# The adaLN modulation of a hybrid trunk layer: two parts as columns on the turned tokens, four parts inside the input projection

## What is computed

```python
mod = silu(c) @ w_ada + b_ada                      # 1024 -> 6 * 1024, for c and for c_ctx
sh1, sc1, g1, sh2, sc2, g2 = split(mod, 6)
h = rms_norm(x, norm1) * (1 + sc1) + sh1
proj = h @ w_in + b_in                             # qa ka va (384 each), qb kb vb ob (384 each), 16 gates, 256 pool
mixed = concat(attention, sigmoid(ob) * mlstm, pool) @ w_out
x = x + g1 * mixed
h2 = rms_norm(x, norm2) * (1 + sc2) + sh2
x = x + g2 * moe(h2)
```

## Time and profile before

| | |
|---|---|
| median of 3 runs | 1669.62 us (1667.91 to 1673.24) |
| profiled execution, its own time | 1669.87 us |
| its span | 1668.2 us |
| TensorE matmuls busy | 1419.5 us, 85% of the span |
| TensorE weight loads | 794.5 us, 48% |
| VectorE busy | 595.0 us, 36% |
| ScalarE busy | 314.8 us, 19% |
| GpSimd busy | 159.3 us, 10% |
| bytes moved by DMA | 222.54 MB, mean 133 GB/s |

### The profile page before, as it was taken

The page is one execution under the profiler, slowest core; times in us unless marked ns, Lnnn a source line. Parts: engine busy times, 40 slices in busy tenths (PEclk is TensorE's granted clock), DMA queues, the critical chain, the costliest instruction groups (busy, mean ns, idle before and its releaser), DMA issues. The chain is left out here.

```text
span 1668.2 us, 16922 instructions
## 1 busy us (share of the span) xinstructions
PE 1419.5 (85%) x5847; PEld 794.5 (48%) x5848; DVE 595.0 (36%) x1173; ACT 314.8 (19%) x681; POOL 159.3 (10%) x167
## 2 busy tenths in 40 slices
PE   5798999999988999866769975079998999999952
PEld 1124555555567788755634432044444444444521
DVE  0242136011111666568922246322232332323217
ACT  0310000033001444433511111011111111111123
POOL 0003000000000111025200000410001000000030
PEclk9998999999998999968979987589999999999977
DMA  8767411110003221001060025337758669577144
GB/s 318 252 239 240 44 38 38 38 38 3 25 33 71 36 39 20 21 11 58 2 239 0 0 63 206 131 130 264 259 203 326 236 237 318 207 278 280 38 180 178
DMA packets 121015, 222.54 MB, mean 133 GB/s; under 512 B 38217, under 2 KB 48121, under 8 KB 120829
## 3 DMA queue, kind: packets, MB, share of 16 engines
q1 hardware_dynamic: 104995, 172.16, 31.3%
q0 software_dynamic: 9664, 32.30, 5.5%
q10 hardware_dynamic: 6304, 17.37, 2.8%
HBM read 194.31 MB, written 30.43 MB: 135 GB/s over the span
## 5 line engine op out<-in xcount | busy, mean ns | idle before, releaser
L485 PE MATMUL ps<-sb 128*128 128x512 f32 (+1 forms) x576 | 189.5, 492 | 1.9 <-PEq L314 1.9
L488 PE MATMUL ps<-sb 128*128 128x384 f32 (+1 forms) x576 | 172.8, 463 | 0.0
L485 PEld LDWEIGHTS ps<-sb 128*128 128x128 f32 x576 | 95.8, 192 | 96.3 <-issue 95.8
L488 PEld LDWEIGHTS ps<-sb 128*128 128x128 f32 x576 | 109.2, 190 | 62.3
L1669 PE MATMUL ps<-sb 128*128 x256 | 120.9, 628 | 13.4 <-ACT sb L1713 13.4
L1229 PE MATMUL ps<-sb 128*128 128x512 f32 x288 | 126.3, 597 | 0.0
L1642 PE MATMUL ps<-sb 128*128 x256 | 115.3, 604 | 1.2 <-ACT sb L1701 1.2
L1646 PE MATMUL ps<-sb 128*128 x256 | 112.5, 592 | 0.0
L209 PE MATMUL ps<-sb 128*2 128x512 f32 x192 | 88.7, 618 | 25.9 <-DMA sb<-in_w_ada 17.3
L1749 DVE TENSOR_SCALAR sb<-sb 128x512 f32<-128x512 f32 (+1 forms) x32 | 11.5, 359 | 270.3 <-ACT sb L1706 236.9
L1229 PEld LDWEIGHTS ps<-sb 128*128 128x128 f32 x288 | 54.7, 192 | 65.9 <-issue 65.9
(11 more groups left out here) (295 smaller groups left out, 1745.4 us busy)
## 6 DMA issues: line engine op xcount, KB each, us to landing
sb<-in_w_gate SPq DMA_DIRECT2D x16, 2048.0 KB, 8.5
sb<-in_w_up SPq DMA_DIRECT2D x16, 2048.0 KB, 15.9
sb<-in_w_down SPq DMA_DIRECT2D x32, 1024.0 KB, 10.0
sb<-in_w_ada SPq DMA_DIRECT2D x12, 2048.0 KB, 8.0
sb<-in_w_in SPq DMA_DIRECT2D x7, 1536.0 KB, 7.1
slot_y<-sb ACTq DMA_DIRECT2D x16, 512.0 KB, 6.5
sb<-mod_rows SPq DMA_DIRECT2D x6, 1024.0 KB, 11.2
sb<-in_x_all ACTq DMA_DIRECT2D x9, 512.0 KB, 6.5
```

Of the source, the lines that this page charges most:

```text
L485: last = nc.tensor.matmul(bank(i % 8)[0:m, 0:tn], w[:, k, b * m:(b + 1) * m], hT[:, k, t0:t0 + tn], start=(k == 0), stop=(k == KD - 1))
L488: last = nc.tensor.matmul(bank(i % 8)[:, 0:m], hT[:, k, t0:t0 + P], w[:, k, 0:m], start=(k == 0), stop=(k == KD - 1))
```

## The change

- The vectors c, b_ada's first 2048 elements and norm1 come in as rows of 128 and are turned once to columns.
- Parts 0 and 1 are made as columns: the 128x128 blocks of w_ada's first 2048 columns are stationary, the two columns of silu(c) move. w_ada comes in eight row blocks of 1 MB with four semaphores; block k from the fifth on waits for the product of block k - 4.
- The token tiles come in three transfers of three. Each batch is squared, scaled by its inverse root in place, turned, and copied by ScalarE and VectorE half each.
- Scale and shift are then applied to `hT`, whose partitions are channels: eight passes over 1024 latent columns (three on ScalarE, five on VectorE), and eight over the 128 context columns.
- All this is at the head of the projection's block; blocks 1 and 2 are gone.
- Parts 2 to 5 are made in eleven pieces of up to 384 columns, inserted as units 12, 16, 20 and so on. A piece is four column groups of 32 stationary columns (two of them are used) and 96 moving columns each. Each piece's weights go to `w_first`, free after qa. The results go to `mod_rows` as they come.
- The order of the groups becomes qa, ka, va, qb, vb, ob, kb, tail, and the sigmoid's work moves under kb. `rpb_rows` is written once unit 8 is done.
- The scale of the second norm is made from the repeated rows in the output projection.

```diff
-        def multiply_ada(pe, n):
-            pe.wait_ge(ada_loaded[n % 2], 16 * (n // 2 + 1))
...
-                last = nc.tensor.matmul(bank(2 + n % 2)[0:2], cc[:, :, k], ada[n % 2][:, k, :],
-                                        start=(k == 0), stop=(k == KD - 1))
...
+        groups = [("T", C_QA, AW), ("T", C_KA, AW), ("N", C_VA, AW), ("S", C_QB, MW), ("N", C_VB, MW), ("N", C_OB, MW),
+                  ("S", C_KB, MW), ("N", C_TAIL, TAIL)]
+        GATE_GROUP = 5
+        PIECE = 4 * 96
+        n_pieces = -(-4 * D // PIECE)
+        piece_cols = lambda j: min(PIECE, 4 * D - j * PIECE) // 4
...
+        for j in range(n_pieces):
+            units.insert(NT + 3 + 4 * j, ("mod", j, 4 * 32, 0, piece_cols(j)))
...
+        early = [sb[:, early_at[k % 7]:early_at[k % 7] + 2 * D] for k in range(KD)]
...
+            for k in range(KD):
+                if k >= 4:
+                    sp.wait_ge(ada_mm, k - 3)
+                sp.dma_start(early[k], w_ada[k * P:(k + 1) * P, 0:2 * D]).then_inc(ada_in[k % 4], 16)
+                if k in (0, 2, 4):
+                    load_x(k // 2)
+            sp.dma_start(w_first, w_src[:, :, C_QA:C_QA + AW]).then_inc(w_first_in, 16)
+
+        def front_act(act):
+            st = act_steps.on(act)
+            act.dma_start(ident, k_ident).then_inc(const_ready, 16)
+            act.wait_ge(vec_copied, 1)
+            nc.scalar.activation(ce, vec_cols[:, 0:2 * KD], ACT.Exp, scale=-1.0).then_inc(silu_exp, 1)
+            for n in range(3):
+                act.wait_ge(x_in[n], 16)
+                tiles = range(BATCH1 * n, BATCH1 * (n + 1))
+                for t in tiles:
+                    if t:
+                        act.wait_ge(squares, t)
+                    nc.scalar.activation(sq_junk, x_res[:, t, :], ACT.Square, accum_out=ss[:, t:t + 1]).then_inc(squares, 1)
+                b = slice(BATCH1 * n, BATCH1 * (n + 1))
+                act.wait_ge(mean_ready, n + 1)
+                nc.scalar.activation(y0[:, b], ss[:, b], ACT.Sqrt).then_inc(guess_ready, 1)
+                for t in tiles:
+                    act.wait_ge(turned, t + 1)
+                    nc.scalar.activation(hT[:, 4:8, t * P:(t + 1) * P], bank(2 * (t % 3) + 1).rearrange("p (k t) -> p k t", k=4),
+                                         ACT.Copy).then_inc(copied_act, 1)
...
+            for k in DVE_KS:
+                nc.vector.tensor_scalar(hT[:, k, 0:LAT], hT[:, k, 0:LAT], mods[:, KD + k, 0:1], mods[:, k, 0:1],
+                                        ALU.mult, ALU.add).then_inc(mod_dve, 1)
...
+            def multiply_ada(k):
+                pe.wait_ge(ada_in[k % 4], 16 * (k // 4 + 1))
+                for b in range(2 * KD):
+                    last = nc.tensor.matmul(bank(6)[:, 2 * b:2 * b + 2], early[k][:, b * P:(b + 1) * P], cc[:, k, 0:2],
+                                            start=(k == 0 and b == 0), stop=(k == KD - 1 and b == 2 * KD - 1))
+                last.then_inc(ada_mm, 1)
+
+            def turn_x(n):
+                for t in range(BATCH1 * n, BATCH1 * (n + 1)):
+                    pe.wait_ge(scaled, t + 1)
+                    if t >= 3:
+                        pe.wait_ge(copied_act, t - 2)
+                        pe.wait_ge(copied_dve, t - 2)
+                    for k in range(KD):
+                        at = 2 * (t % 3) * BANK + k * P
+                        last = nc.tensor.transpose(ps[:, at:at + P], x_res[:, t, k * P:(k + 1) * P], ident)
+                    last.then_inc(turned, 1)
+
+            for step in (0, 1, 2, "x0", 3, "x1", 4, 5, "x2", 6, 7):
...
+                for i in range(len(units)):
...
+                            sp.dma_start(wring[g % 2][:, :, 0:n], w_src[:, :, c0:c0 + n]).then_inc(w_loaded[g % 2], 16)
+                    if i == last_of[0]:
+                        sp.dma_start(rpb_rows, bass.AP(rpb_pad.tensor, 0, [[PADW, HEADS * RPB_R], [0, GRID_W], [1, PADW]])).then_inc(mod_stored[0], 16)
+                    for j in range(n_pieces):
+                        if i == (piece_at[j - 1] if j else last_of[0]):
+                            sp.wait_ge(proj_mm, i + 1)
+                            at, n = 2 * D + j * PIECE, 4 * piece_cols(j)
+                            sp.dma_start(w_piece[:, :, 0:n], ada_src[:, :, at:at + n]).then_inc(piece_in, 16)
...
+                    if g == "mod":
+                        pe.wait_ge(piece_in, 16 * (b + 1))
+                        for k in range(KD):
+                            for q in range(4):
+                                last = nc.tensor.matmul(bank(i % 8)[32 * q:32 * q + 32, 0:tn], cc[:, k, :], w_piece[:, k, q * tn:(q + 1) * tn],
+                                                        start=(k == 0), stop=(k == KD - 1))
+                        last.then_inc(proj_mm, 1)
+                        continue
...
+                dve.wait_ge(n2_rows_in, 48)
+                st.link(nc.vector.scalar_tensor_tensor(out=n2_rows[0], in0=n2_rows[0], scalar=1.0, in1=bc(n2_w[:, None, :], (P, 2, D)),
+                                                       op0=ALU.add, op1=ALU.mult))
                 dve.wait_ge(sq2, 1)
```

More of the change, by code:

```diff
@@ L174, in program @@
         mark_h = ar.at
[L175 to L192, removed]
-        dve_steps, act_steps = Steps(None, sem("dve_steps")), Steps(None, sem("act_steps"))
[L194 to L202, removed]
-        def multiply_ada(pe, n):
-            pe.wait_ge(ada_loaded[n % 2], 16 * (n // 2 + 1))
-            if n >= 2:
-                pe.wait_ge(mod_evac, n - 1)
-            for k in range(KD):
-                last = nc.tensor.matmul(bank(2 + n % 2)[0:2], cc[:, :, k], ada[n % 2][:, k, :],
-                                        start=(k == 0), stop=(k == KD - 1))
[L211 to L222, removed]
+        dve_steps, act_steps = Steps(None, sem("dve_steps")), Steps(None, sem("act_steps"))
+        mod_stored = [sem("mod_stored0"), sem("mod_stored1")]
         def newton(st, y, t, ms):
@@ L229, in newton @@
             st.link(nc.vector.scalar_tensor_tensor(out=y, in0=t, scalar=1.5, in1=y, op0=ALU.add, op1=ALU.mult))
[L231 to L287, removed]
@@ L299, in load_rows_of, with norm_stage @@
                 sp.dma_start(row, mod_row(part)).then_inc(loaded, 16)
[L301 to L311, removed]
+        def norm_stage(tag, x, rinv, nat, outT, sp_more, pe_more, dve_last, pool_more, rows):
+            (scale_row, shift_row), row_loaded = rows
             nat_ready, turned, copied = (sem(tag + n) for n in ("nat_ready", "turned", "copied"))
-            nat_of = lambda t: two[t % 2] if ring else nat[:, t, :]
             with nc.Block() as block:
@@ L316, in _ @@
                 def _(sp):
[L317 to L320 removed]
+                    sp_more(sp)
                 @block.scalar
@@ L423, in program @@
         after_attention_in = ar.at
+        pin_at = ar.at
         pin = ar.take([NT, PW])
@@ L451, in program @@
         sig_exp, zeros_ready = sem("sig_exp"), sem("zeros_ready")
+        x_res = sb[:, mark_h:mark_h + NT * D].rearrange("p (t d) -> p t d", t=NT)
+        early_at = [after_proj, after_proj + KD * AW] + [kaT_at + n * 2 * D for n in range(3)] + [mark_h + NT * D + n * 2 * D for n in range(2)]
+        assert early_at[-1] + 2 * D <= qaT_at and early_at[4] + 2 * D <= pin_at
+        early = [sb[:, early_at[k % 7]:early_at[k % 7] + 2 * D] for k in range(KD)]
+        small = Arena(sb, after_proj)
@@ new lines, in program @@
+        small.at = pin_at
+        vec_rows, vec_cols = small.take([P]), small.take([40])
+        ce, cc = small.take([2 * KD]), small.take([KD, 32])
+        mods = small.take([2 * KD, 2])
+        ss, y0, nt1 = (small.take([NT]) for _ in range(3))
+        brow = small.take([n_pieces * (PIECE // 4)])
+        mrow = [small.take([PIECE // 4]) for _ in range(2)]
+        sq_junk = sb[:, block_at:block_at + D]
+        vec_in, vec_turned, vec_copied, silu_exp, silu_done = (sem(n) for n in ("vec_in", "vec_turned", "vec_copied", "silu_exp", "silu_done"))
```

217 lines of the change are left out of this document (143 added, 74 removed).

## The result

The changed kernel takes 1630.63 us (median of 4 runs, 1626.49 to 1635.64) against 1669.60 us (1667.91 to 1673.24): a ratio of 0.977, 95% interval 0.974 to 0.980.

The account below looks back on a forecast made before the run. Data and TensorE together bound the front, TensorE alone the projection. Terms: -59.5 + 48 + 18.5 + 1.1 = +8.1 us against 1669.87, so 1678 us; own range 1671 to 1685, eight in ten 1653 to 1689.

Parts of the forecast that it names:

- front, start of the projection: Before the projection: two-column products at 213 ns and transposes let it start at 73.6 instead of 133.1, 59.5 us gained.
- pieces in the projection: Eleven inserted pieces, 704 records at 65 ns on gapless TensorE plus 0.1 us at each piece end: 48 us added.
- wait for piece 0: SP's queue: the rpb_rows write after unit 8 delays piece 0's load; 16 us wait plus 2.5 slow clock, 18.5 added.
- behind the projection: Output projection: a VectorE pass over 2 x 1024 columns ahead of the mean, partly in idle time, 1.1 us added.
- I take 65: Pieces in the projection: the issue rate of load and matmul pairs sets 65 ns a record, 45.8 us for 704.
- rival 1: Pieces' four groups issue at the weight-load bound, 27 ns: 21 us in place of 48, so 1651; chance 0.14.
- Rival 2: SP's queue overlaps piece 0 with the table, so no wait: 1659.5 us; chance 0.13.
- Rival 3: Front runs at the full clock: projection at 50 us, 83 gained, so 1654.5; chance 0.09.

Follow-up runs that it names:

- one_group: Changed kernel with all four parts of a piece sent to one column group, same records and columns: 1673.02 us, ratio 1.001.
- probe: Rows of small matrix instructions added after the projection's last unit, executed once, only steps read: 63 ns transposing, 125 plain, 9 to 10 in four groups.
- table_late: Changed kernel with the write of rpb_rows made to wait for unit 8, piece 0's load directly behind it: 1656.99 us, 24.6 above the unedited changed kernel.

## Why the prediction was wrong, point by point

| term | forecast | measured |
|---|---|---|
| front, start of the projection | 73.6 us, -59.5 | 75.81 us, -57.3 |
| pieces in the projection | +48 | +18.1 |
| wait for piece 0 | +18.5 | 0 |
| behind the projection | +1.1 | +3.0, of which VectorE 0.8 |
| span | +8.1 | -36.2 |

**The pieces: a limit that isn't there, and so a term mis-sized.** It was right that they sit on TensorE's path, that the groups overlap (one_group) and that a change of shape costs some 0.2 us a piece. The step that failed is "Then the rate at which pairs of load and matmul can be issued decides" with its "I take 65", taken from L1348's nine transposes. I read that row as the rate at which pairs can be issued. It was the step of one kind of instruction: a transposing record with a 128-column load, 63 ns in the probe. The measured record is 22.8 ns, 15.6 us for all, where I had 45.8. The other 2.5 of the 18.1 are some 0.2 us by which the units between two pieces take longer (15.7 us in place of the 15.5 of the earlier trace rows), and 0.5 us of slow clock at the projection's start, 65.3 to piece 0 in place of 64.8. 22.8 lies below the 27 of rival 1, because my quarter of 107 ns for a 32-column load was no floor either: L535 goes at 9 to 10. It is close to a quarter of the 84 ns of one group, which is what full overlap gives. Rival 1 was right about the full overlap and wrong about the load as its bound, and I gave it 0.14. The rows that were like a piece, L1615's two column groups, said "fully overlapped" and nothing spoke against carrying that on to four; I set a row of another instruction against them.

**The wait for piece 0: a step misread.** "Now it is issued when unit 8 is done" is wrong. In the code, the write of `rpb_rows` stands under the test for `last_of[0]`, but the wait on `proj_mm` stands only inside the branches for a w_in group and for a piece. An `if` on the unit's number sets the place in the queue's order, not a time. SP therefore reached the table at once, at 75.08. The rest of this step held: with a wait in front of it the table does hold piece 0 back, by 22.4 us and 2.8 of slow clock (table_late), where I had 16 and 2.5: the table's rate is 100 GB/s and not 113. Rival 2 gave "no wait", though for another reason than the true one.

**The front: right.** Products at 213 ns were forecast. The first 96 took 215, where the clock's column reads 1.00 and the clock is inferred; behind the transposes they took 206 to 215 at a granted 0.50. Their end was forecast at 72.1 and was 72.05. Within it two errors cancel. The start came 0.7 late and TensorE waited 2.25 us for a batch of tokens; against this the three groups of transposes brought back 32 x (215 - 126) + 64 x (215 - 176) + 64 x (215 - 165) ns = 8.5 us, where I had 6. The 2.2 us by which the projection is late are the first scale-and-shift pass: 3.14 us behind GpSimd's memset, where 3.71/5 = 0.74 was to be had. I had looked at what VectorE does there and not at what GpSimd does. Rival 3 (full clock) did not occur: the 106 ns step lasted a few us behind each group of transposes. That the end came out to 0.05 us is partly luck.

**The rest.** The sigmoid under the units of kb cost nothing. In the output projection the new pass is one instruction, here with what follows:

```profile
946.48 2.28 DVE L1327 SCALAR_TENSOR_TENSOR sb<-sb 128x2048 f32<-128x2048 f32 x1
948.80 0.17 DVE L1330 TENSOR_SCALAR sb<-sb 128x9 f32<-128x9 f32 x1
```

The idle 1.45 us ahead of the mean is gone. From the start of the last addition to the mean it takes 2.93 us instead of 2.14: +0.8, forecast +1.1. The other 2.2 us behind the projection lie within the spread of single executions (9 us in what is behind the last group), and I have not followed them.

With the two failed terms replaced by what was measured, my own sum is -59.5 + 18 + 1.1 = -40.4, or 1629.5 us; the median is 1630.6.

## What to carry to other kernels

Price an instruction by a row of the same kind, with the same load width and the same placing in the array; the smallest step seen of another kind is no floor. Before you forecast a wait, find the line of the wait in the queue's program: a position in a loop orders an issue, but doesn't delay it. And try a product with two useful rows in four column groups with a wide moving operand: here that started the projection 26 us sooner than 256 records of two columns did. Read the clock's column together with the steps; at the head of these profiles it says 1.00 where the steps are those of 0.50.

## What the runs showed of the hardware

- An f32 record with 32 stationary and 96 moving columns goes every 81 to 84 ns in one column group and every 23 in four; with 16 moving columns every 31 to 32 and every 9 to 10.
- Two-column matmuls behind 128-column loads lose the full clock while TensorE is busy without a gap: 105 ns a step becomes 211 (probe). Wide transposes between them brought the short step back three times.
- With the same shape and load a transposing record goes every 63 ns and one of a plain f32 matmul every 125 at a mean granted clock of 0.90 (probe).
- A copy from DRAM to DRAM in packets of 508 bytes runs alone at 99 to 102 GB/s, and a load of 1.5 MB issued right behind it on the same queue lands only after 36.8 us.
- VectorE's operation on 16 columns took 4.47 us while GpSimd filled 6912 and then 1056 columns, and 0.17 without; a pass over 1024 took 3.14 behind a memset of 3.01.
